# Attention gates in a hybrid HGRN2 and differential-attention step: rows through DRAM in place of diagonal matrices and products with ones

## The reference, cut to what matters

```python
def modulation(cvec, w_ada, b_ada):
    m = jax.nn.silu(cvec) @ w_ada + b_ada
    return jnp.split(m, 6, axis=-1)
...
        xp = xp + g1p * yp          # yp, ys: output of the token mixer
        xs = xs + g1s * ys
...
        xp = xp + g2p * hier_moe(hp, ...)
        xs = xs + g2s * hier_moe(hs, ...)
```

## Time and profile before

| | |
|---|---|
| Median of 3 runs | 1179.23 us (1174.76 to 1180.16) |
| Profiled execution, its own time | 1178.38 us |
| Its span, first to last instruction | 1176.6 us |
| TensorE busy | 95% of the span |
| VectorE, ScalarE, GpSimd busy | 35%, 19%, 11% |
| Mean granted TensorE clock | 0.984 of 2.4 GHz |
| Moved by DMA | 321 MB, 273 GB/s in the mean |

### The profile page before, as it was taken

How to read it: one execution, slowest core, us unless ns; L and a number is a source line. 1 busy time by engine, 2 the same in 40 slices (tenths; PEclk the granted TensorE clock), 3 DMA queues, 4 the chain that set the end, 5 groups by cost and what they waited for, 6 DMA issues and landing times.

```text
span 1176.6 us, 19792 instructions
## 1 busy us (share of the span) xinstructions
PE 1112.5 (95%) x8488; PEld 659.8 (56%) x8488; DVE 414.4 (35%) x1058; ACT 229.1 (19%) x530; POOL 127.7 (11%) x226
## 2 busy tenths in 40 slices
PE   4999999998999999999998899989989899999996
PEld 1666666665444676666663444434545756666552
DVE  2155555556712340000113654307753330000105
ACT  3111101101211411111112311116632411111110
POOL 0343433333100000000001000000000000000003
PEclk9999999999999989999999899998999899999999
DMA  9985444446941579999999910088760789999995
GB/s 346 307 274 153 125 144 145 145 144 216 373 166 69 189 288 421 414 426 424 429 423 330 389 39 1 18 337 317 253 256 10 258 334 420 427 424 425 426 418 219
DMA packets 102463, 321.26 MB, mean 273 GB/s; under 512 B 4048, under 2 KB 39168, under 8 KB 87008
## 3 DMA queue, kind: packets, MB, share of 16 engines
q1 hardware_dynamic: 93872, 298.05, 66.4%
q0 software_dynamic: 3248, 10.87, 2.8%
q10 hardware_dynamic: 5248, 10.98, 2.4%
HBM read 305.73 MB, written 14.16 MB: 272 GB/s over the span
## 4 chain that ended last, share of the span: by engine, by line
PE 81%; DMA 8%; DVE 4%; issue 2%; ACT 2%; SPq 2%; POOL 0%; POOLq 0%; ACTq 0%; DVEq 0%
PE bank L771 17%; PE bank L924 11%; PE bank L1119 11%; PE bank L794 7%; PE bank L661 7%; PE bank L760 6%; DMA ring<-in_moe_w_down 5%; PE bank L933 4%; PE bank L1050 4%; PE bank L556 3%; PE bank L949 2%; PE bank L640 1%; PE bank L647 1%; DMA ring<-in_w_ada 1%; DMA ring<-expert_rows,moe_row 1%
## 5 line engine op out<-in xcount | busy, mean ns | idle before, releaser
L771 PE MATMUL bank<-ring,xn 128*64 128x256 f32 x1472 | 163.5, 380 | 0.6 <-DMA ring<-in_moe_w_up 0.6
L771 PEld LDWEIGHTS bank<-ring,xn 128*64 128x64 f32 x1472 | 105.0, 137 | 61.1 <-issue 9.5
L924 PE MATMUL bank<-uT,ring 128*128 128x384 f32 x384 | 135.0, 496 | 0.0
L1119 PE MATMUL bank<-ring,uT 128*128 128x512 f32 x288 | 129.8, 605 | 5.2 <-DMA ring<-in_attn_w_qkv 3.5
L1833 DVE TENSOR_TENSOR moe_hh<-xn,bank 128x256 f32<-128x256 f32 x32 | 13.5, 421 | 291.9 <-ACT xn L1312 291.8
L794 PE MATMUL bank<-ring,xn 128*64 128x512 f32 x384 | 106.7, 596 | 0.9 <-ACT xn L1318 0.9
L1119 PEld LDWEIGHTS bank<-ring,uT 128*128 128x128 f32 x288 | 54.4, 194 | 70.4 <-issue 65.5
L924 PEld LDWEIGHTS bank<-uT,ring 128*128 128x128 f32 x384 | 69.2, 190 | 41.3 <-issue 1.1
L760 PE MATMUL bank<-moe_g,moe_h 128*128 128x128 f32 x672 | 84.6, 285 | 0.3 <-DVE moe_g L1723 0.3
L661 PE MATMUL bank<-ring,uT 128*128 128x512 f32 x192 | 84.0, 593 | 0.0
L760 PEld LDWEIGHTS bank<-moe_g,moe_h 128*128 128x128 f32 x672 | 80.9, 199 | 5.2 <-issue 5.2
(11 more groups left out here) (293 smaller groups left out, 1294.3 us busy)
## 6 DMA issues: line engine op xcount, KB each, us to landing
ring<-in_w_ada SPq DMA_DIRECT2D x24, 2048.0 KB, 11.6
ring<-in_moe_w_up SPq DMA_DIRECT2D x24, 2048.0 KB, 18.8
ring<-in_moe_w_gate SPq DMA_DIRECT2D x22, 2048.0 KB, 17.6
ring<-in_moe_w_down SPq DMA_DIRECT2D x21, 2048.0 KB, 22.2
ring<-in_hgrn_w_in SPq DMA_DIRECT2D x32, 512.0 KB, 7.7
moe_ring<-in_moe_w_gate SPq DMA_DIRECT2D x8, 2048.0 KB, 19.1
moe_ring<-in_moe_w_up SPq DMA_DIRECT2D x8, 2048.0 KB, 23.2
moe_ring<-in_moe_w_down SPq DMA_DIRECT2D x7, 2048.0 KB, 19.9
```

Source lines behind the costliest of these rows:

```text
L771: last = mm(bank[2 + e][64 * g:64 * g + 64, 256 * part:256 * part + 256], m["xe"][:, k, 64 * e:64 * e + 64], w[k][:, 256 * g:256 * g + 256 ...
L924: last = mm(to[:, 0:TOK], w[:, k, f, :], uT[:, k, :], start=(k == 0), stop=(k == KC - 1))
L1119: last = mm(bank[b % 2][:, :], uT[:, k, t * P:(t + 1) * P], cols(slot)[:, k, :], start=(k == 0), stop=(k == KC - 1))
```

## The change

In both layers the twelve instructions that spread the gate behind the mixer (4 on VectorE, 4 on TensorE, 4 on ScalarE) are gone. In their place, `store_gates` writes blocks 4 and 5 of `adaln` to a DRAM tensor `gate_rows` of 2 x 1024 by two transfers, one for each vector, each of 1024 pieces of 4 bytes; `load_gates` waits for both and then reads the two rows onto all 128 partitions of `gates` by one transfer of 1 MB. In layer 0 ScalarE issues them, the stores after head 3 and the load after head 5. In layer 1 GpSimd issues them, between the two layers' experts, where it waits for block 5 of layer 1's modulation. `update_x` waits for the load. The semaphores of the gates count 4 quarters in place of 8 in each layer.

```diff
+        gates_in = ((c_and_gates, 32), (late_in, LATE))
...
+        def store_gates(eng, n):
+            need(eng, n, "mod_cols", 6)
+            with nc.allow_non_contiguous_dma(reason="gate rows by feature"):
+                for c in range(2):
+                    eng.dma_start(gate_rows[n][c].rearrange("(k p) -> p k", p=P),
+                                  adaln[:, n, 4:6, :, c].rearrange("p b j -> p (b j)")).then_inc(gates_in[n][0], 16)
+        def load_gates(eng, n):
+            eng.wait_ge(*gates_stored(n))
+            eng.dma_start(gates[:, :, :], gate_rows[n].partition_broadcast(P)).then_inc(gates_in[n][0], 16)
...
             g_tile(0, 0)
-            gate(0, HG["diag"], 0, 0, 2)
             g_tile(0, 1)
-            gate(0, HG["diag"], 0, 1, 3)
             g_tile(1, 0)
             g_tile(1, 1)
-            gate(0, HG["diag"], 0, 2, 2)
             pe.wait_ge(hg["gated"], 2)
             turn_tile(0, "oT_done", xn, 0, (0, 1))
-            gate(0, HG["diag"], 0, 3, 3)
...
             attend(len(units) - 1)
-            gate(1, AT["mod"], 0, 0, 6)
-            gate(1, AT["mod"], 0, 1, 7)
             for t in range(2):
                 pe.wait_ge(at["o_ready"], t + 1)
                 turn_tile(1, "oT_done", xn, t, (2 * t, 2 * t + 1))
             out_tile(1, 0, 0)
-            gate(1, AT["mod"], 0, 2, 6)
-            gate(1, AT["mod"], 0, 3, 7)
             out_tile(1, 0, 1)
...
                 rest_out(i * 2 + 1, 1, i)
+                if i == 1:
+                    store_gates(act, 0)
+                elif i == 2:
+                    load_gates(act, 0)
...
                 need(dve, n, "out_mm", m + 1)
-                need(dve, n, "gate_ready", half + 1 if t == 0 else 4)
+                dve.wait_ge(*gates_loaded(n))
...
             experts(0)
+            store_gates(pool, 1)
+            load_gates(pool, 1)
             experts(1)
```

More of the change, by code:

```diff
@@ L330, in trunk @@
         token_table = [nc.dram_tensor(f"token_table{n}", (TOK, D), F32, kind="Internal").ap() for n in range(2)]
+        gate_rows = [nc.dram_tensor(f"gate_rows{n}", (2, D), F32, kind="Internal").ap() for n in range(2)]
         HG, AT, MOE = mem["hgrn"], mem["attn"], mem["moe0"]
@@ L633, in late_turn, with gate @@
                 turn_mod(1, EARLY + h, AT["mod"], h % 2, 5, h + 1)
-            def gate(n, raw, which, q, to):
-                need(pe, n, "diag", 4 * which + q + 1)
+            def gate(n, raw, q, to):
+                need(pe, n, "diag", q + 1)
                 if q >= 1:
-                    need(pe, n, "gate_ready", 4 * which + q)
+                    need(pe, n, "gate_ready", q)
                 mm(bank[to][:, :], ones, raw[:, q % 2, :], start=True, stop=True).then_inc(S[n]["gate_mm"], 1)
@@ L833, in body @@
                         pe.wait_ge(s["passes_ready"], 1)
-                        gate(n, m["diag"], 1, 0, 6)
+                        gate(n, m["diag"], 0, 6)
                     gate_up(i, 0, 1, it)
                     if gating:
-                        gate(n, m["diag"], 1, 1, 6)
+                        gate(n, m["diag"], 1, 6)
                     if last:
@@ L844, in body @@
                     if gating:
-                        gate(n, m["diag"], 1, 2, 6)
+                        gate(n, m["diag"], 2, 6)
                     gate_up(i, 1, 1, it)
@@ L849, in body @@
                     if gating:
-                        gate(n, m["diag"], 1, 3, 6)
+                        gate(n, m["diag"], 3, 6)
                     pe.wait_ge(s["h_ready"], it * 2 + 2)
@@ L1238, in raw_out, with gate_out @@
                 A(raw[:, b, :], bank[to][:, :], ACT.Copy).then_inc(S[n]["mod_raw"], 1)
-            def gate_out(n, which, q, src):
+            def gate_out(n, q, src):
                 c, half = divmod(q, 2)
-                need(act, n, "gate_mm", 4 * which + q + 1)
+                need(act, n, "gate_mm", q + 1)
                 A(gates[:, c, 512 * half:512 * half + 512], bank[src][:, :], ACT.Copy).then_inc(S[n]["gate_ready"], 1)
@@ L1580, in columns, with gate_diagonal @@
                     .then_inc(S[n]["mod_ready"], steps)
-            def gate_diagonal(n, raw, part, which, q):
+            def gate_diagonal(n, raw, part, q):
                 c, half = divmod(q, 2)
                 if q >= 2:
-                    need(dve, n, "gate_mm", 4 * which + q - 1)
+                    need(dve, n, "gate_mm", q - 1)
                 v.tensor_tensor(raw[:, q % 2, :].rearrange("p (j m) -> p j m", j=4),
@@ L1812, in body @@
                     if gating:
-                        gate_diagonal(n, m["diag"], 5, 1, 0)
-                        gate_diagonal(n, m["diag"], 5, 1, 1)
+                        gate_diagonal(n, m["diag"], 5, 0)
+                        gate_diagonal(n, m["diag"], 5, 1)
                     if first:
```

43 lines of the change are left out of this document (15 added, 28 removed).

## The result

The changed kernel takes 1181.11 us in the median of 20 runs, against 1177.11 us for the kernel before in 20 runs beside it. The ratio is 1.0040, with a 95% interval of 1.0025 to 1.0055: 0.4% slower, where 0.7% faster was forecast. One of the 20 executions took 1643.76 us at a granted clock of 0.653; the ratio leaves it out. The profiled execution's span is 1181.3 us, 4.7 more than before.

A forecast was written before the change was run, and what follows sets the result against it. TensorE bounds the kernel, on the chain for 81% of the span. 3.58 + 4.72 - 0.1 = 8.2 us gained, giving 1170.6 us, 0.7% faster; range 1166 to 1175, with the rivals 1165 to 1177.

The forecast's parts named there:

- What is removed: Gate products and their diagonals and copies in both layers: 3.58 us gained in layer 0, 4.72 in layer 1.
- second pair: Layer 1, gate products behind the first output tile, with ScalarE's copy between them: 2.73 us gained, all on the chain.
- First pair: Layer 1, from last head output to first output product: 1.99 us gained, bounded by VectorE's head norm.
- the 0.1 us taken off for it: Layer 1's gain reduced because TensorE's lower clock would cover the turning and a little of the first output product.
- The weight stream: Layer 0's experts: stream expected to move earlier by the whole gain; rival, chance 0.12, that it keeps the gain: 1173.8 us.
- the term for the price of the stores: Both layers' 4-byte stores to DRAM, no such write in the trace: taken as 0 us.
- cost 0: Layer 0's two store issues on ScalarE: between 1.8 and 11.0 us, lower end taken, so no delay to `hg_q`.
- The two issues on ScalarE: Layer 0, after head 3, in a 10.35 us idle gap before the `hg_q` copy: no cost; upper end 0.7 us late.
- The second rival: Small pieces hold the DMA queues, late weights delay TensorE; chance 0.10; gain cancelled at 12.9 us, 101 ns a piece.
- the load that the text priced: Layer 1's late modulation weights issued at 824.9, landed at 834.4, used at 839.07: 4.7 us of slack.
- A DMA wait before a late product: Sign against the prediction: late modulation products should stay evenly apart, with no DMA wait before one.
- 41 ns a piece: Second rival's bound from loads of short pieces: one layer's stores take up to 5.2 us on the queues.

The follow-up runs named there:

- without stores: Changed kernel without its stores in either layer, gate rows loaded from `b_ada` instead: 1168.21 us, 0.9922 of the kernel before.
- The kernels with one layer alone: New way of making the gates in one layer, the other as before the change: layer 0 alone 1177.66 us, 0.9997; layer 1 alone 1184.71 us, 1.0054.
- the 64-byte runs: Changed kernel with one store a layer in runs of 64 bytes, `update_x` reading its gate with a stride: 1173.37 us, 0.9957.
- One store alone: Changed kernel with rows from `b_ada`, no stores in layer 0, one store of 1024 4-byte pieces in layer 1: 1175.37 us, 0.9997.
- the two that nobody waited for: Rows from `b_ada`, no layer 0 stores, layer 1's two stores issued behind the last late weights, at block 11: 1168.26 us, 0.9924.
- the one with two stores in layer 1: Changed kernel with rows from `b_ada`, no stores in layer 0, two stores in layer 1 that nobody reads: 1177.84 us, 1.0013.
- those four kernels: Changed kernel (1181.11 us), new way in layer 0 alone (1177.66), and rows from `b_ada` with two (1168.65) or four (1172.04) stores in layer 0 only.
- the one with the longest gap: New way of making the gates in layer 0 alone, layer 1 as before the change: 1177.66 us, 0.9997.

## Why the prediction was wrong

*What is removed* was right. Layer 0: the same stretch from head 7's `kbT` copy to the first `update_x` is 59.31 us before (300.36 to 359.67) and 55.73 without stores (300.29 to 356.02), 3.58 less, as forecast to the hundredth. Layer 1, second pair: the 2.73 us are gone. First pair: 7.83 became 6.29, a gain of 1.54 where 1.99 less 0.1 was forecast. The lower clock (0.54 to 0.60 from 874 to 878 us) lay over the turning, whose 16 products took 3.41 us and now stand on the chain, where VectorE's head norm was expected. From the last head output to the end of the first tile's 32 products it is 24.54 us before and 20.02 after, so 4.52 of the 4.62 us forecast were gained. In the kernel without stores that stretch has 21.46 us, since the lower clock (0.50 from 856 to 864 us) lay over the first products too (14.91 in place of 13.73): where the lower level falls moves this gain by more than the 0.1 us taken off for it. The weight stream kept little of layer 0's gain: without stores the chain's wait at the end of layer 0's experts has 31.63 us, 0.74 more than in the earlier trace rows, and starts at 591.28, 6.5 us earlier (2.9 us of that are not the gate's, and no run says whose). After the change the same 31.63 us start at 597.15.

*The step that failed* is the term for the price of the stores, put at nothing: "The stores' price is unseen in this trace", followed by "I take 0", and with it layer 0's "cost 0". Its measure is 13.9 us for both layers (1.0040 less 0.9922). Measured apart, in kernels of their own, layer 1's two stores cost 10.7 us, clear of the noise, and layer 0's 2.9, which is not. The kernels with one layer alone fit: layer 0's, 3.6 of gain less 2.9, should be 0.7 us faster and is 0.4; layer 1's, 10.7 less the 4.3 gained there (1.54 + 2.73), 6.4 slower, and is 6.4. That they fit to tenths is luck, with intervals of some 5 us. The two issues on ScalarE cost nothing, as forecast: `hg_q` comes 11.44 us behind head 3's `kbT` copy, 11.43 before. In the account of the one trace, layer 1's part is 8.27 us of wait for the late weights and 2.6 for the clock behind it; layer 0's is 1.75 us more between heads 3 and 4. Head 7 is 0.8 us longer (27.65 us, 26.85 before), but it is 27.08 without stores and 28.49 with the 64-byte runs, so no run ties this to the close pieces. Another 1.3 us of layer 0 were there at head 0 already (`kbT` at 83.93, before at 82.61), ahead of everything that was changed, and so belong to the execution.

*Why it failed.* The second rival had the mechanism, the place and nearly the break-even point: small pieces, late modulation weights 4.7 us from being late, and at 12.9 us of hold the gain cancelled. (The load that came late is the one before the load that the text priced. By its 8.6 us before and its product due at 829.46 it had 5.6 us of slack, and was 14 us longer on its way.) One store alone landed after 9.8 us, the two that nobody waited for after 11.5 and 14.0. A DMA wait before a late product was among the signs that the text named. The rival was given 0.10 because its price was bounded by reads of short pieces, 41 ns a piece on a queue, and it was thought of as a price by the piece. Both were wrong. The bound from reads did not hold for these writes: one store, 64 pieces a queue, landed after 9.8 us, up to 153 ns a piece. And the price is not by the piece alone: it hangs on how close in DRAM the pieces lie. The page "DMA: Bandwidth & Descriptors" of the Trainium skill, section "Specifications", with pieces under 512 bytes read, modified and written, stood beside the sum and was given no weight in it. Its direction was right. The 512 bytes, which it gives for the full rate, are not what decided here: 4-byte pieces 64 bytes apart, eight of them in 512 bytes, were cheap, as were runs of 64 bytes.

*What the forecast left out.* For the layer-0 stores the text named what waits for ScalarE and for the load, and not what else is on the queues. It had no stage in which TensorE loses time behind slower queues without waiting at a semaphore. And a slack of 4.7 us is small beside the spread of an unseen price.

Open: why the first 1024 close pieces cost 8.8 us and the next 1024 only 1.9 (their number, or their place behind the late load), in blocks of what size they clash, and what TensorE waits for in layer 0.

## What to carry to other kernels

When data with one number a partition must go to DRAM as a row, turn it first (here 0.27 us of TensorE and 0.25 us of ScalarE for 2048 numbers) and store runs; a transfer of 4 KB in 4-byte pieces can take longer than one of 2 MB (9.8 us to landing for one store, 8.6 for a late load before the change). Price a transfer by what shares the queues with it, and read a window's GB/s beside its share: a store that nobody waits for is free only while nothing else on the queues has little slack, as the same two stores 40 us later were. And when the one price that a forecast lacks has no row of its own kind, the bound from another kind is no bound, and the range must not lean on it.

## What the runs showed of the hardware

4-byte writes to DRAM that lie within 64 bytes of each other slow the other transfers on the core's queues: 25 to 48 GB/s in all, in place of up to 393, for about 10 us behind 2048 such pieces in the changed kernel and in the one with two stores in layer 1. When the pieces lie 512 bytes apart the slow stretch is 4 us. In layer 0 TensorE stood for 0.7 to 2.9 us without a semaphore in that time. In three of those four kernels an instruction load of 16 KB took 2.2 to 2.7 us in place of 1; the one with the longest gap has none. ScalarE's issues of four such stores took 16.2 us in all, up to 10.46 us for one, where two took 0.41 and 0.61.

VectorE multiplied 128 x 512 in 1.02 us when one operand had a stride of 64 bytes, in 0.69 us when it was contiguous.
